# Recurrence levels made by VectorE alone, with an absolute value on ScalarE, in a two-block model kernel on one core

## The reference, cut to what matters

```python
def step(state, inp):                       # one chunk of 64 tokens
    qi, ki, vi, gi = inp
    bcum = jnp.cumsum(gi, axis=2)           # gi: log of the forget gate, <= 0
    o_inter = jnp.einsum('bhtk,bhkv->bhtv', qi * jnp.exp(bcum), state)
    rel = bcum[:, :, :, None, :] - bcum[:, :, None, :, :]
    decay = jnp.exp(jnp.where(incl, rel, -jnp.inf))
    scores = jnp.einsum('bhtk,bhsk,bhtsk->bhts', qi, ki, decay)
    o_intra = jnp.einsum('bhts,bhsv->bhtv', scores, vi)
    ...
    return state, o_inter + o_intra
```

## Time and profile before

| what | value |
|---|---|
| median of 3 runs | 3291.14 us (3289.87 to 3292.67) |
| the profiled execution | 3294.34 us, its span 3293.0 us |
| mean granted TensorE clock in it | 0.951 of full speed |
| PE busy | 2984.3 us, 91% of the span |
| DVE busy | 1606.7 us, 49% |
| ACT busy | 1012.4 us, 31% |
| POOL busy | 347.1 us, 11% |
| table loads of ScalarE | 51, 65.4 us |

### The profile page before, as it was taken

The page is one execution under the profiler, slowest core; times in us unless marked ns, Lnnn a source line. Parts: engine busy times, 40 slices in busy tenths (PEclk is TensorE's granted clock), DMA queues, the critical chain, the costliest instruction groups (busy, mean ns, idle before and its releaser), DMA issues.

```text
span 3293.0 us, 44283 instructions
## 1 busy us (share of the span) xinstructions
PE 2984.3 (91%) x18450; PEld 2404.6 (73%) x18450; DVE 1606.7 (49%) x3113; ACT 1012.4 (31%) x1950; POOL 347.1 (11%) x606
## 2 busy tenths in 40 slices
PE   7988899999999998788699999999899798699998
PEld 4657688889977566677557888888656687478886
DVE  3122444444446255776864424333825566655354
ACT  2011432233343155333233212111426344232222
POOL 0000000000000100543500000000110244200001
PEclk9999999999999999899799999999999798899999
DMA  5423241222222110222422121121111010222321
GB/s 180 149 98 128 83 122 40 58 58 67 69 96 103 51 33 1 81 77 79 152 93 86 42 77 65 52 71 70 39 45 33 17 33 20 90 90 79 114 85 69
DMA packets 227299, 246.62 MB, mean 75 GB/s; under 512 B 5552, under 2 KB 193052, under 8 KB 225564
## 3 DMA queue, kind: packets, MB, share of 16 engines
q1 hardware_dynamic: 227100, 243.79, 23.0%
HBM read 234.34 MB, written 9.44 MB: 74 GB/s over the span
## 4 chain that ended last, share of the span: by engine, by line
PE 54%; DVE 9%; ACT 4%; issue 2%; DMA 1%; POOL 1%; ACTq 0%; DVEq 0%; POOLq 0%; SPq 0%
PE PS L2048 51%; PE PS L2052 2%; PE PS L2257 2%; ACT AR L174 1%; DVE AR L2776 1%; DVE AR L2767 1%; ACT L169 1%; DVE AR L3012 1%; DVE STAT L2948 0%; DVE EX L2999 0%; ACT EX L174 0%; DMA WR<-in_w_in 0%; DVE AR L2785 0%; ACT STAT L174 0%; DVE AC L3004 0%
## 5 line engine op out<-in xcount | busy, mean ns | idle before, releaser
L2048 PE MATMUL PS<-HI,WC 128*128 128x512 f32 (+2 forms) x1600 | 428.0, 353 | 0.6 <-DVE WC L2993 0.6
L2048 PE MATMUL PS<-AR 128*64 128x64 f32 (+8 forms) x3756 | 322.1, 271 | 73.7 <-ACT AR L174 18.8
L2048 PE MATMUL PS<-HT,WR 128*128 128x256 f32 (+3 forms) x1136 | 355.3, 467 | 21.0 <-ACT EX L174 5.8
L2048 PE MATMUL PS<-WR,HT 128*128 128x256 f32 (+2 forms) x1744 | 364.0, 366 | 11.4 <-ACT AR L174 5.6
L2048 PEld LDWEIGHTS PS<-AR 128*64 128x64 f32 (+5 forms) x3756 | 278.1, 175 | 125.8 <-issue 49.8
L2048 PE MATMUL PS<-DW,DH 128*128 128x384 f32 (+1 forms) x1344 | 357.0, 348 | 0.9 <-DVE AR L2631 0.9
L174 ACT ACTIVATE AR<-PS 128x256 f32<-128x256 f32 (+3 forms) x389 | 165.7, 453 | 623.2 <-PE PS L2048 477.0
L2048 PEld LDWEIGHTS PS<-WR,HT 128*128 128x128 f32 x1744 | 282.2, 199 | 77.5 <-issue 41.5
L2048 PEld LDWEIGHTS PS<-HI,WC 128*128 128x128 f32 x1600 | 284.0, 189 | 42.3 <-DVE WC L2993 1.1
L2048 PEld LDWEIGHTS PS<-HT,WR 128*128 128x128 f32 (+2 forms) x1136 | 213.6, 194 | 130.7 <-issue 90.2
L2048 PE MATMUL PS<-LO,WC 128*128 128x512 f32 (+2 forms) x800 | 282.2, 353 | 0.0
(11 more groups left out here) (344 smaller groups left out, 4548.0 us busy)
## 6 DMA issues: line engine op xcount, KB each, us to landing
WR<-in_w_ffn_in SPq DMA_DIRECT2D x40, 1024.0 KB, 7.0
WR<-in_w_in_b SPq DMA_DIRECT2D x51, 512.0 KB, 5.9
WR<-in_w_mod SPq DMA_DIRECT2D x12, 2048.0 KB, 7.9
WR<-in_w_mod SPq DMA_DIRECT2D x24, 1024.0 KB, 5.4
WR<-in_w_ffn_out SPq DMA_DIRECT2D x22, 1024.0 KB, 5.0
WR<-in_w_in SPq DMA_DIRECT2D x40, 512.0 KB, 4.3
WR<-in_w_out SPq DMA_DIRECT2D x8, 2048.0 KB, 9.2
WR<-in_w_in_a SPq DMA_DIRECT2D x8, 1024.0 KB, 5.3
```

Source lines behind the costliest of these rows:

```text
L2048: mm = lambda o, l, r, start, stop: e.o.matmul(o, l, r, start=start, stop=stop, skip_group_check=True)
```

## The change

Six edits, in words:
1. hl1: VectorE alone subtracts ref from all 256 columns of a level (7 instructions on 256 columns), so the k halves come out with the wrong sign; GpSimd's hl1 is gone. ScalarE first takes the absolute value of the 1792 columns in place, waits for it, and then takes exp(-x).
2. hl2: VectorE alone multiplies all 256 columns (7 instructions), with an operand that takes the k half from one 768-column piece and the q half from the next; GpSimd's hl2 is gone. For this the set of a head is laid out with q between the two k.
3. hl4: the tensor_reduce is replaced by three additions (levels 0-2 plus 3-5: 384 columns; 0-1 plus 2 and 6: 256; 0 plus 1: 128), each waiting for the one before.
4. In the second layer units 0, 1 and 2 of head 0 are begun and weighed in the attention, instead of unit 0 alone; after the fence hl1 of unit 1 and `recur`'s hl2 and hl1 of units 1 and 2 are not added again. In the first layer this stays as it was.
5. `FILL` of the second layer goes from 0.88 to 0.92.
6. The semaphores of hl2's two halves become one.

```diff
-        def levels_early(H):
+        def levels_early(H, ahead):
             H.units = units(H)
-            levels_begin(H, 0)
-            yield
-            levels_weigh(H, 0)
-            yield
-
-        def levels_first(H):
-            levels_multiply(H, 0)
-            levels_begin(H, 1)
+            for u in range(ahead + 1):
+                if u < ahead:
+                    levels_begin(H, u)
+                if u:
+                    levels_weigh(H, u - 1)
+                yield
...
-            H.lv[u]["weighed"] = [("hl_p", n), ("hl_q", n)]
+            H.lv[u]["weighed"] = [("hl_w", n)]
...
-                if u + 1 < len(H.units):
+                if u + 1 < len(H.units) and "weighed" not in H.lv[u + 1]:
                     levels_weigh(H, u + 1)
-                if u + 2 < len(H.units):
+                if u + 2 < len(H.units) and u + 2 not in H.lv:
                     levels_begin(H, u + 2)
...
-        RATE, FILL, MODS = ((1, 2, 2, 1), (1.4, 2.5, 2.5, 1)), ((0.45, 0.69), (0, 0.88)), (1.4, 1.4, 2.2, 2.6)
+        RATE, FILL, MODS = ((1, 2, 2, 1), (1.4, 2.5, 2.5, 1)), ((0.45, 0.69), (0, 0.92)), (1.4, 1.4, 2.2, 2.6)
...
-                sets.append((t6[0], t6[1:3], t6[3:5], t6[5].rearrange(...), t6[6].rearrange(...)))
+                sets.append((t6[1], [t6[0], t6[2]], t6[3:5], (X if b_ else EX)[:, 0:3840], t6[5].rearrange(...), t6[6].rearrange(...)))
...
+                H.beside = [KQ, KQ[:, 768:3840]]
...
-            first = itertools.chain(prepare(heads[0]), levels_early(heads[0]))
+            first = itertools.chain(prepare(heads[0]), levels_early(heads[0], 1 if both else 3))
...
-            levels_first(heads[0])
+            levels_multiply(heads[0], 0)
+            if both:
+                levels_begin(heads[0], 1)
...
 (ScalarE)
             def hl1(n, H, i, d, xb, until):
                 x = xb[0:H.K, :]
                 e.wait_ge("hl_b", n)
-                e.wait_ge("hl_k", n)
-                e.activation(x, x, ACT.Exp).then_inc(sem("hl_e"))
+                e.activation(x, x, ACT.Abs).then_inc(sem("hl_a"))
+                e.wait_ge("hl_a", n)
+                e.activation(x, x, ACT.Exp, scale=-1.0).then_inc(sem("hl_e"))
...
 (VectorE, hl1)
-                    ref = b4[:, :, 1, 0:1] if rev else b4[:, :, 0, h - 1:h]
-                    s = tt(v(x3[:, l, :])[:, :, 0 if rev else 1, :], b4[:, :, 0 if rev else 1, :], ref.broadcast_to([K, 128 // h, h]), ALU.subtract)
+                    n3 = lambda a: a.rearrange("p (n m) -> p n m", m=2 * h)
+                    ref = (b4[:, :, 1, 0:1] if rev else b4[:, :, 0, h - 1:h]).broadcast_to([K, 128 // h, 2 * h])
+                    s = tt(n3(x3[:, l, :]), n3(lg[:, lo:hi]), ref, ALU.subtract)
...
 (VectorE, hl2)
                 for l in range(7):
-                    v = lambda a: a.rearrange("p (n t h) -> p n t h", t=2, h=64 >> l)[:, :, 0 if rev else 1, :]
-                    m = tt(v(x3[:, l, :]), v(x3[:, l, :]), v(H.q[:, 128 * i:128 * i + 256]), ALU.mult)
-                m.then_inc(sem("hl_q"))
+                    h = 64 >> l
...
+                    kq = H.beside[rev][0:H.K, 128 * i:128 * i + 2 * (768 + h)].rearrange("p (t m) -> p t m", t=2)[:, :, 0:256]
+                    m = tt(x4, x4, kq.rearrange("p t (n s h) -> p t n s h", s=2, h=h)[:, :, :, 0, :], ALU.mult)
+                m.then_inc(sem("hl_w"))
...
 (VectorE, hl4)
-                m4 = M.rearrange("p (t l n) -> p t n l", t=2, l=8)
-                e.o.tensor_reduce(Am.rearrange("p (t n) -> p t n", t=2), m4[:, :, :, 0:7], AX, ALU.add).then_inc(sem("hl_r"))
+                tt(m4[:, :, 0:3, :], m4[:, :, 0:3, :], m4[:, :, 3:6, :], ALU.add).then_inc(sem("hl_s"))
+                e.wait_ge("hl_s", 2 * n - 1)
+                tt(m4[:, :, 0:2, :], m4[:, :, 0:2, :], m4[:, :, 2:7:4, :], ALU.add).then_inc(sem("hl_s"))
+                e.wait_ge("hl_s", 2 * n)
+                tt(Am.rearrange("p (t n) -> p t n", t=2), m4[:, :, 0, :], m4[:, :, 1, :], ALU.add).then_inc(sem("hl_r"))
...
 (GpSimd: its hl1 and hl2, written like VectorE's for the other half, are removed)
```

More of the change, by code:

```diff
@@ L1603, in build @@
                 t6 = [get(n) for n in range(7)]
-                sets.append((t6[0], t6[1:3], t6[3:5], t6[5].rearrange("p (i n) -> p i n", i=6), t6[6].rearrange("p (i n) -> p i n", i=6)))
+                sets.append((t6[1], [t6[0], t6[2]], t6[3:5], (X if b_ else EX)[:, 0:3840], t6[5].rearrange("p (i n) -> p i n", i=6), t6[6].rearrange("p (i n) -> p i n", i=6)))
             late_arenas = [Arena(at=LT_AT, size=base), Arena(at=base + 1536, size=early_at)]
@@ L1609, in build @@
             w1, third = wslots[1], late_arenas[1].get(768)
-            sets.append((w1[:, 0:768], [w1[:, 768 * j:768 * j + 768] for j in (1, 2)], [w1[:, 768 * j:768 * j + 768] for j in (3, 4)],
+            sets.append((w1[:, 768:1536], [w1[:, 768 * j:768 * j + 768] for j in (0, 2)], [w1[:, 768 * j:768 * j + 768] for j in (3, 4)], w1[:, 0:3840],
                          third.rearrange("p (i n) -> p i n", i=6), BR[:, :, 384:512]))
@@ L1636, in project @@
             def project(h, prr=prr, slots=None, after=None, both=both, l=l, sets=sets, heads=heads, th=th, set_until=set_until):
-                QF, KF, LG, VH, GH = sets[h % 3]
+                QF, KF, LG, KQ, VH, GH = sets[h % 3]
                 H = heads[h]
@@ L1742, in ended @@
                     heads[h].ended = True
-                    set_until[h % 3] = (("hoe", P.count["hoe"]), ("ho", P.count["ho"]), ("hl_p", heads[h].weighed), ("hl_q", heads[h].weighed))
+                    set_until[h % 3] = (("hoe", P.count["hoe"]), ("ho", P.count["ho"]), ("hl_w", heads[h].weighed))
                 yield from recur(heads[h], ended)
@@ L2774, in hl2 @@
                 for l in range(7):
-                    v = lambda a: a.rearrange("p (n t h) -> p n t h", t=2, h=64 >> l)[:, :, 0 if rev else 1, :]
-                    m = tt(v(x3[:, l, :]), v(x3[:, l, :]), v(H.q[:, 128 * i:128 * i + 256]), ALU.mult)
-                m.then_inc(sem("hl_q"))
+                    h = 64 >> l
+                    x4 = x3[:, l, :].rearrange("p (n t h) -> p n t h", t=2, h=h)
+                    kq = H.beside[rev][0:H.K, 128 * i:128 * i + 2 * (768 + h)].rearrange("p (t m) -> p t m", t=2)[:, :, 0:256]
+                    m = tt(x4, x4, kq.rearrange("p t (n s h) -> p n t s h", s=2, h=h)[:, :, :, 0, :], ALU.mult)
+                m.then_inc(sem("hl_w"))
             def hl4(n, H, d, L, M, m_until, Am, a_until):
@@ L3030, in hp2 @@
                 tt(qh, H.q, qh, ALU.mult).then_inc(sem("hp_p"))
-            def hl1(n, H, i, d, xb, until):
-                k, lg, rev, order = H.dirs[d]
-                K = H.K
-                x3 = xb[0:K, :].rearrange("p (l n) -> p l n", l=7)
-                lo, hi = 128 * i, 128 * i + 256
-                e.wait_ge(*H.cum[d])
-                e.wait_all(until)
-                for l in range(7):
-                    h = 64 >> l
-                    v = lambda a: a.rearrange("p (n t h) -> p n t h", t=2, h=h)
-                    b4 = v(lg[:, lo:hi])
-                    ref = b4[:, :, 1, 0:1] if rev else b4[:, :, 0, h - 1:h]
-                    s = tt(v(x3[:, l, :])[:, :, 1 if rev else 0, :], ref.broadcast_to([K, 128 // h, h]), b4[:, :, 1 if rev else 0, :], ALU.subtract)
-                s.then_inc(sem("hl_k"))
-            def hl2(n, H, i, d, L):
-                k, lg, rev, order = H.dirs[d]
-                x3 = L["xb"][0:H.K, :].rearrange("p (l n) -> p l n", l=7)
-                e.wait_ge(*L["exped"])
-                for l in range(7):
-                    v = lambda a: a.rearrange("p (n t h) -> p n t h", t=2, h=64 >> l)[:, :, 1 if rev else 0, :]
-                    m = tt(v(x3[:, l, :]), v(x3[:, l, :]), v(k[:, 128 * i:128 * i + 256]), ALU.mult)
-                m.then_inc(sem("hl_p"))
             def g2(n, g):
@@ L3067, in rj @@
                 tt(o, a, b, ALU.add).then_inc(sem("rj"))
-            return dict(fence=fence, rj=rj, hp2=hp2, hl1=hl1, hl2=hl2, g2=g2, an=an, dump=dumped(e))
+            return dict(fence=fence, rj=rj, hp2=hp2, g2=g2, an=an, dump=dumped(e))
         def sp_program(e):
```

5 lines of the change are left out of this document (3 added, 2 removed).

## The result

| | before | after |
|---|---|---|
| median of 12 runs | 3291.78 us (3288.50 to 3293.72) | 3296.68 us (3294.05 to 3301.27) |
| ratio | | 1.0017, 95% interval 1.0009 to 1.0025 |
| span of the profiled execution | 3293.0 us | 3298.4 us |
| VectorE / ScalarE / GpSimd busy | 1606.7 / 1012.4 / 347.1 us | 1586.9 / 1078.7 / 93.5 us |

The change makes the kernel slower: 4.9 us by the medians, 5.6 us (0.17%) by the ratio. The forecast was 3296.4, plus 5.3, so the number came out. Several steps on the way to it did not, and their errors cancel; the experiments tell how far.

A forecast was written before the change was run, and what follows sets the result against it. TensorE, busy 91%, was taken to bound the kernel, VectorE its tails. First layer -1.9 and second +7.2 gave +5.3: 3299.6 us from the profiled 3294.34, or 3296.4 against the median 3291.14; range 3280 to 3305.

The forecast's parts named there:

- the two waits near 2676 and 2694: Second layer's middle: TensorE waits for copies behind absolute values and exponentials on ScalarE, +3.5 and +3.6 us.
- that sign of its own: Second layer's attention: the forecast is wrong if it does not get longer; its fence was to come about 6 us later.
- Prices: Per instruction group, all units: seven 256-column instructions 2.45 us, absolute value 1.70, three additions 1.35 for a 1.72 reduction.
- The stall of up to 0.85 us per unit behind the exponential: Where VectorE is the bound: it stalls up to 0.85 us before hl2; +3.5 us in the first tail.
- nothing gained: hl4, by the skill's rule: reduction 0.99 us, additions 0.98; as a rival about 3300 us, chance 0.05.
- Nobody waits for what it keeps: GpSimd, whole kernel: it loses its level work and no engine waits for its remaining work; no cost counted.
- First layer: Sum of the first layer, -1.9 us: end of attention +0.8, TensorE's waits in the middle +1.6, tail -4.3.
- Second layer's attention: Early hl1 and hl2 of units 1 and 2 pass through the last two jobs: fence +6.2 us, bounds 0 and +11.
- After the fence: Second layer: TensorE's 5.59 us wait for hl2 of unit 1 goes, projections' first weights come +0.7 late: -4.9 us.
- rival of ScalarE's queue: Middle stretches: TensorE's copies behind a unit's exponential come 1.7 us later, six more places +10; about 3306 us, chance 0.17.
- The second tail: End of the second layer's recurrence: VectorE has 14 us of pause in 60; hl4 and hl2 give -1.2 us.
- the faster rival: Second layer: early units fit the attention's holes, absolute values overlap projections; -8.0 us, about 3283, chance 0.31.

The follow-up runs named there:

- b_fill92: Kernel before with only the second layer's FILL at 0.92 instead of 0.88: 3282.4 us, ratio 0.9976 to the kernel before.
- a_late92: Changed kernel with only unit 0 begun and weighed in the second attention, FILL kept at 0.92: 3299.6 us, ratio 1.0023 to the kernel before.
- a_late: Changed kernel with the second layer's order put back, unit 0 alone early and FILL 0.88: 3309.6 us, ratio 1.0053 to the kernel before.
- a_noabs: Changed kernel with the absolute value left out, one exponential at scale -0.001: 3273.2 us, ratio 0.9950 to the kernel before.
- b_early: Kernel before with units 0, 1 and 2 early in the second attention and FILL 0.92: 3283.2 us, ratio 0.9974 to the kernel before.
- a_halves: Changed kernel with hl1 as fourteen signed 128-column VectorE subtractions, no absolute value: 3279.5 us, ratio 0.9966 to the kernel before.
- a_split1: Changed kernel with hl1 split between VectorE and GpSimd as before, no absolute value: 3276.9 us, ratio 0.9959 to the kernel before.

## Why the prediction was right, and where it was not

The time was right by luck. In the second layer two steps came out 10 us better than forecast and three steps 12 us worse, and the stretches that the change does not touch lie some 3 us apart in the two executions. Of the signs that the prediction named, the two waits near 2676 and 2694 came. But the second attention did not get longer, and by that sign of its own the forecast's account was wrong. By steps:

- **Prices.** Seven on 256 columns: 2.45 forecast (its own sum, 1.50 + 0.92, is 2.42), 2.43 and 2.50 measured with GpSimd quiet. Absolute value 1.70, measured 1.69. Additions 1.35, measured 1.35 with GpSimd quiet. The stall of up to 0.85 us per unit behind the exponential: in the two tails seven hl2 wait 0.46 to 1.30 us, 6.2 us in all. The Trainium skill's rule in "VectorE: DVE Perf Modes", section on the TRN2 errata, put the additions at an estimated 0.98 us in all; the three rows give 0.56 + 0.43 + 0.29 = 1.28 busy, 0.3 more; for the reduction that they replace it is 0.7 too low (1.72 measured, 0.99 by the rule), and that is why its "nothing gained" did not come true per unit. The same section calls that rule too low for a single instruction and gives (N + 151) cycles at 0.96 GHz for an fp32 tensor_tensor of N columns: an estimated 0.56, 0.42 and 0.29 us for 384, 256 and 128 columns, which the rows bear out.
- **"Nobody waits for what it keeps"** of GpSimd failed. The prices forecast 40 x (0.45 + 0.35) = 32 us less of VectorE; its level work fell by 18 (327 to 309 us busy). The ten instructions that ran into GpSimd's products cost it some 16 us. Two of these places have TensorE waiting: after the first fence, and at 1568.94 in the first tail (2.47 us for hl2).
- **First layer**, -1.9 forecast, -1.0 measured by the shift. Its attention +1.5 for +1.4. After the fence +1.0 for -0.65: TensorE waits 6.50 us for hl2, longer than the 5.47 before. The absolute value, which I had left out of that chain, makes VectorE wait 0.89 us in front of hl2, and hl2 then takes 4.10 in place of 3.42, since its last multiplication runs into GpSimd's product. Middle +1.5 for +1.6, with the two waits of 5.14 now 6.27 and that at 1467 down from 3.02 to 2.43. Tail -6.7 for -4.3, by other terms: hl2 gave 2.7 us where 6.3 were forecast, hl4 2.6 for 2.4, and the 3.3 us that VectorE had waited for TensorE's products fell to 0.6, which was not in the sum; hl2's stalls, 3.1 for 3.5, were right. The rest of the 6.7 was not told apart. Behind the tail a wait for weights from memory (1.36, now 2.26) and 0.9 us at 1658 give back 1.7.
- **Second layer's attention**, +6.2 forecast, -0.8 measured. The step that failed is the sum of this stage, which had the early units as its only term. That term was right: with FILL 0.92 on both sides the early units move the fence by +6.3 and +6.0. What failed is that edit 5 was put at nothing. Alone it moves the fence by -7.6 (b_fill92), and the edits on the levels add 0.8 to that (a_late92, -6.8): -7.6 + 0.8 + 6.0 = -0.8. I had read FILL as part of the early units' order and gave it no price.
- **After the fence**, -4.9 forecast, -7.9 measured: the wait of 5.59 us, and hl3 of unit 1 at full clock soon after (0.98 us for 28 matmuls that took 1.73). So edit 4 gives after the fence about what it takes ahead of it. With FILL 0.92 it is worth 2 us by the times in the changed kernel and nothing in the one before, both within the intervals.
- **The two waits for ScalarE**, +3.5 and +3.6 forecast. They came where they were forecast and for the reason given, with 3.2 and 2.7 us of wait, and 1.1 at 2684. Mis-sized was the clock, which the sum took as 0: 2.9 and 1.7 us behind these two waits. Together +11.7 for +7.1.
- **A third wait**, at 2738.86, was not in the sum: two units' absolute values and exponentials in one row on ScalarE (6.73 us) ahead of two copies for TensorE, +4.2 with its clock, and +0.6 more up to 2758. It was in the rival of ScalarE's queue, one of its "six more" places. By that rival's sign, waits of over 1 us for ScalarE in the middle stretches, there were four before and are seven now.
- **The second tail**, -1.2 forecast, +1.4 measured. hl2 waits 2.6 us for ScalarE in it, which may be most of it; no run takes this apart.

So the sum for the edits on the levels was 4 and is 17 (a_late); the sum for edits 4 and 5 was 1 and is -12. The absolute value is the whole loss and more: without it the same kernel is 0.5% faster than before (a_noabs), twice what the faster rival had. Of that, 8 us are edit 5 (b_fill92), and 8 more (0.9950 against b_early's 0.9974) are what VectorE alone gives once ScalarE is not made to pay. a_noabs computes something else, but a_halves and a_split1 compute what the changed kernel does, and they keep 17 and 19 of the 22 us.

Open: how much of the absolute value's 22 us is half clock and how much wait, beyond the three places read above. The first layer's part (some 12 us of shift against a_noabs) is spread over about ten places and was not told apart.

## What to carry to other kernels

An instruction moved to an engine that is busy 31% is not free: ask at each place what copy for the bound engine stands behind it in the same queue, count two instructions where two units come in a row, and add the matmuls that run at half clock after the wait, which cost up to as much again as the wait here. An engine that has been relieved is still in the way with what it keeps: look where its last long instructions fall. A changed number in a table of rates is an edit with a price of its own, to be measured alone before anything is credited to the edit beside it. A sum that comes out right is not a proof of its terms.
